# Context rows, first products and the ends of two mixer projections in another order, in a two-layer block

## The reference

```python
silu_c, silu_cc = silu(c), silu(c_ctx)
for i in range(2):                               # layer 0: attention, layer 1: Fourier mixing
    sh1, sc1, g1, sh2, sc2, g2 = split(silu_c @ ada_w[i] + ada_b[i], 6)       # six vectors of 2048
    h = modulate(rms_norm(x, norm_mix_g[i]), sh1, sc1)                        # x: 256 x 2048
    if i == 0:
        h_ctx = modulate(rms_norm(ctx, norm_mix_g[0]), csh1, csc1)            # context: 256 x 2048
        q, k, v = project_qkv(h, attn_w_qkv);  k_c, v_c = project_kv(h_ctx, attn_w_qkv[:, 2048:])
        o = latent_attention(rope(q), rope(k), v, k_c, v_c) @ attn_w_o        # 16 heads, 4 for k and v
    else:
        o = fourier_mix(h) @ fourier_w_o                                      # 8 groups of 256 channels
    x = x + g1 * o
    x = x + g2 * square(relu(modulate(rms_norm(x, norm_mlp_g[i]), sh2, sc2) @ mlp_w1[i])) @ mlp_w2[i]
return rms_norm(x, final_norm_g)
```

## Time and profile before

| | us |
|---|---|
| median of 3 runs (lowest, highest) | 2068.01 (2066.21, 2069.05) |
| the profiled execution | 2064.34 |
| its span, first to last instruction | 2062.5 |
| TensorE busy (matmuls) | 1995.7 |
| VectorE busy | 1364.1 |
| ScalarE busy | 971.5 |

### The profile page before, as it was taken

How to read it: one execution, slowest core, us unless ns; L and a number is a source line. 1 busy time by engine, 2 the same in 40 slices (tenths; PEclk the granted TensorE clock), 3 DMA queues, 4 the chain that set the end, 5 groups by cost and what they waited for, 6 DMA issues and landing times.

```text
span 2062.5 us, 25228 instructions
## 1 busy us (share of the span) xinstructions
PE 1995.7 (97%) x10356; PEld 1630.1 (79%) x10356; DVE 1364.1 (66%) x1373; ACT 971.5 (47%) x1268; POOL 110.6 (5%) x196
## 2 busy tenths in 40 slices
PE   4999989998999999999999999899999999999998
PEld 2677756687888888888888787788888888888886
DVE  1456888758868788677568778766656555455546
ACT  4433555445455445544444443445445554444444
POOL 1111001100000000000000001000000000000000
PEclk8999999999999999999999999999999999999999
DMA  9799758966989899688678739767776565555553
GB/s 369 275 333 353 272 215 300 342 208 224 342 309 337 329 347 377 224 327 322 213 275 352 265 105 344 265 226 248 253 250 230 186 204 189 199 187 201 207 202 122
DMA packets 153797, 542.81 MB, mean 263 GB/s; under 512 B 9393, under 2 KB 10577, under 8 KB 116177
## 3 DMA queue, kind: packets, MB, share of 16 engines
q1 hardware_dynamic: 120848, 335.77, 46.4%
q0 software_dynamic: 31744, 201.34, 26.4%
q10 hardware_dynamic: 1090, 4.09, 0.5%
HBM read 535.91 MB, written 2.10 MB: 261 GB/s over the span
## 4 chain that ended last, share of the span: by engine, by line
PE 88%; DMA 6%; DVE 4%; ACT 1%; issue 1%; POOL 0%; ACTq 0%; SPq 0%; DVEq 0%; POOLq 0%
PE ps L1797 23%; PE ps L1799 12%; PE ps L1741 11%; PE ps L1744 11%; PE ps L1745 11%; PE ps L1577 4%; PE ps L1578 4%; PE ps L1579 4%; DMA ada_raw<-in_ada_w 3%; DMA raw<-in_fourier_w_o 1%; PE ps L1931 1%; PE ps L1879 1%; PE ps L1618 1%; DVE g_row L1053 1%; DMA c_rows<-in_ctx 1%
## 5 line engine op out<-in xcount | busy, mean ns | idle before, releaser
L1025 DVE TENSOR_TENSOR w_lo<-raw,w_hi 128x1024 fp32r<-128x1024 f32 x616 | 748.5, 1222 | 530.6 <-ACT w_hi L624 530.4
L624 ACT ACTIVATE w_hi<-raw 128x1024 fp32r<-128x1024 f32 x616 | 648.7, 1059 | 867.7 <-PE ps L1745 345.4
L1797 PE MATMUL ps<-hh,w_hi 128*128 128x512 f32 x2048 | 723.8, 399 | 3.1 <-DVE hh L1390 3.1
L1799 PE MATMUL ps<-hh,w_lo 128*128 128x256 f32 x2048 | 573.6, 280 | 0.0
L1797 PEld LDWEIGHTS ps<-hh,w_hi 128*128 128x128 f32 x2048 | 386.4, 189 | 100.0 <-issue 7.0
L1799 PEld LDWEIGHTS ps<-hh,w_lo 128*128 128x128 f32 x2048 | 387.8, 189 | 0.0
L1741 PE MATMUL ps<-w_hi,hh 128*128 128x512 f32 x992 | 386.2, 389 | 0.4 <-DVE w_lo L1025 0.4
L1745 PE MATMUL ps<-w_hi,hh 128*128 128x512 f32 x992 | 385.9, 389 | 0.0
L1744 PE MATMUL ps<-w_lo,hh 128*128 128x512 f32 x992 | 385.9, 389 | 0.0
L1741 PEld LDWEIGHTS ps<-w_hi,hh 128*128 128x128 f32 x992 | 186.2, 188 | 39.9 <-DVE w_lo L1025 1.3
L1745 PEld LDWEIGHTS ps<-w_hi,hh 128*128 128x128 f32 x992 | 186.2, 188 | 38.9
(11 more groups left out here) (216 smaller groups left out, 1422.2 us busy)
## 6 DMA issues: line engine op xcount, KB each, us to landing
raw<-in_mlp_w SPq DMA_DIRECT2D x256, 1024.0 KB, 5.3
ada_raw<-in_ada_w POOLq DMA_DIRECT2D x151, 1024.0 KB, 6.0
spare<-in_ada_w POOLq DMA_DIRECT2D x30, 1024.0 KB, 7.1
raw<-in_attn_w_qkv SPq DMA_DIRECT2D x24, 1024.0 KB, 10.6
raw<-in_attn_w_o SPq DMA_DIRECT2D x16, 1024.0 KB, 6.4
raw<-in_fourier_w_o SPq DMA_DIRECT2D x16, 1024.0 KB, 8.5
g_row<-in_ada_w POOLq DMA_DIRECT2D x11, 1024.0 KB, 9.4
g_row<-gate_rows SPq DMA_DIRECT2D x48, 64.0 KB, 5.0
```

The costliest lines, as they stand in the source:

```text
L624: act.activation(w_slot(s)[0], raw[:, piece % RAW, s % 2, :], ACT.Copy).then_inc(hi_ready, 1)
L1025: nc.vector.tensor_tensor(lo, raw[:, s // 2 % RAW, s % 2, :], hi.bitcast(F32), ALU.subtract).then_inc(lo_ready, 1)
L1797: mm(ps[:, bank, :].rearrange("p (a t) -> p a t", a=2), w_hi[:, s % SPLIT, w], hh[:, k, :, :], start=(k == 0), stop=False, skip_group_chec ...
L1799: ins = mm(ps[:, bank, 0:T], w_lo[:, s % SPLIT, w], h_hi[:, k, :], start=False, stop=(k == KT - 1), skip_group_check=True)
```

## The change

It changes the order of work at the start and at two ends, and loads a table earlier.

First stage: the context rows are loaded after weight piece 1 instead of piece 0, and GpSimd waits for them before ada_w piece 8. The ada_w pieces stand after other products for the first quarter, their banks are 6, 6, 7, 6, and the context is turned after product 4 in banks 5 and 7. ScalarE makes split 0 first, then shapes x in two halves, then split 1, and TensorE's products can start on the first half. The context's squares, roots and norms move to p = 1, around splits 4 and 5, and the copies of the turned context on VectorE go behind low parts 6 and 7.

Table: a square root of one column, not used, ahead of split 59.

Ends of the two mixer projections: laying out and picking the vector go behind the last product, on either side of tile 0's turns; VectorE takes it up between the last total and its reciprocal; one low part instead of two stands ahead of the last gate, the other behind the first `h_split`.

```diff
@@ -60,7 +60,8 @@
-ADA_AFTER = (1, 2, 4, 5, 7, 8, 10, 11)
+ADA_AFTER = ((2, 3, 4, 6, 7, 9, 10, 11), (1, 2, 4, 5, 7, 8, 10, 11), (1, 2, 4, 5, 7, 8, 10, 11))
+ADA_BANK = (6, 6, 7, 6)
@@ -331,6 +332,8 @@
     gate_in = sem("gate_in")
+    hhi_first = sem("hhi_first")
+    h_first = sem("h_first")
     pick_ready = sem("pick_ready")
@@ -490,7 +493,7 @@
             load_columns(p, wqkv_v[p // 6, column_block(p)])
-            if p == 0:
+            if p == 1:
                 sp.dma_start(c_rows[:, :, :], ctx_in[0].rearrange("(a p) d -> p a d", p=P)).then_inc(ctx_rows_in, 16)
@@ -545,6 +548,8 @@
                 pool.wait_ge(ada_mm, n - 6)
+            if n == 8:
+                pool.wait_ge(ctx_rows_in, 16)
             dst = ring(start_slot(n)).rearrange("p (k c) -> p k c", k=4)
@@ -669,7 +674,18 @@
                 act.wait_ge(col_mm, g)
-            act.activation(ada_rows[:, :], ps[:, 6 + g % 2, :], ACT.Copy).then_inc(rows_copied, 1)
+            act.activation(ada_rows[:, :], ps[:, ADA_BANK[g], :], ACT.Copy).then_inc(rows_copied, 1)
+
+        def shape_first():
+
+            act.wait_ge(a_ready, 1)
+            for half in range(2):
+                kts = slice(2 * half, 2 * half + 2)
+                for kt in range(2 * half, 2 * half + 2):
+                    act.activation(xT[:, kt, :], xT[:, kt, :], ACT.Identity, bias=mod_col[:, kt:kt + 1],
+                                   scale=a_col[:, 0, kt:kt + 1]).then_inc(mod_done, 1)
+                act.wait_ge(mod_done, 2 * half + 2)
+                act.activation(h_hi[:, kts, :], xT[:, kts, :], ACT.Copy).then_inc((hhi_first, hhi_ready)[half], 1)
@@ -727,19 +743,22 @@
         rows_out(0)
-        shape(0, 0)
         split_hi(0)
+        shape_first()
         split_hi(1)
-        for st in range(2, 4):
-            square_in(st)
-            root_in(st)
         split_hi(2)
...
             g, i = p // 6, p % 6
+            if p == 1:
+                square_in(2)
+                root_in(2)
             if p:
...
                 split_hi(2 * p + 3)
+            if p == 1:
+                square_in(3)
+                root_in(3)
             if g < 3 and i == 5:
@@ -826,6 +845,7 @@
                 q_roots(2, 2)
+        act.activation(rst_in[:, 0, 0:1], eps_col[:, 1:2], ACT.Sqrt)
         split_hi(59)
@@ -882,14 +902,16 @@
             else:
-                if q == 2:
-                    act.wait_ge(rows_T, LAID[8] - 5)
-                    act.activation(ada_rows[:, :], ps[:, 2, :], ACT.Copy).then_inc(rows_copied, 1)
                 square_banks(q, 6, 1)
...
                 split_hi(next_first + 1)
+            if q == 0:
+                rows_early(2)
+            if q == 2:
+                act.wait_ge(rows_T, LAID[8] - 5)
+                act.activation(ada_rows[:, :], ps[:, 2, :], ACT.Copy).then_inc(rows_copied, 1)
             square_banks(q, 7, 1)
@@ -925,8 +947,6 @@
                         square_banks(0, i // 8 * 2 + i % 2, 1)
-                    if i == 9:
-                        rows_early(2)
             else:
@@ -1135,7 +1155,7 @@
                 dve.wait_ge(vec_ready, 3)
-            cols = ps[:, 6 + g % 2, 0:16].rearrange("p (m f h v) -> p v m h f", f=2, m=2, h=2, v=2)
+            cols = ps[:, ADA_BANK[g], 0:16].rearrange("p (m f h v) -> p v m h f", f=2, m=2, h=2, v=2)
             for v, dst in enumerate((mod_col, modc_col)):
@@ -1145,6 +1165,13 @@
                                                misc[:, V_MIX + 4 * g:V_MIX + 4 * g + 4], ALU.add, ALU.mult).then_inc(a_ready, 1)
+
+        def lower_first(half):
+
+            kts = slice(2 * half, 2 * half + 2)
+            dve.wait_ge((hhi_first, hhi_ready)[half], 1)
+            nc.vector.tensor_tensor(h_lo[:, kts, :], xT[:, kts, :], h_hi[:, kts, :].bitcast(F32),
+                                    ALU.subtract).then_inc((h_first, h_ready)[half], 1)
@@ -1224,26 +1251,29 @@
         split_lo(0)
+        lower_first(0)
+        lower_first(1)
         split_lo(1)
-        lower(0, 0)
-        total_in(2)
-        normed_in(2)
-        total_in(3)
-        normed_in(3)
         split_lo(2)
...
             g, i = p // 6, p % 6
+            if p == 1:
+                total_in(2)
+                normed_in(2)
+            if p and p != 20:
+                split_lo(2 * p + 2)
+                split_lo(2 * p + 3)
+            if p == 1:
+                total_in(3)
+                normed_in(3)
             if p == 2:
...
                     nc.vector.tensor_copy(ctxT[:, 2 * k:2 * k + 2, :],
-                                          ps[:, 4 + k % 2, :].rearrange("p (a t) -> p a t", a=2)).then_inc(ctx_T_out, 1)
-            if p and p != 20:
-                split_lo(2 * p + 2)
-                split_lo(2 * p + 3)
+                                          ps[:, 5 + 2 * (k % 2), :].rearrange("p (a t) -> p a t", a=2)).then_inc(ctx_T_out, 1)
             if p == 3:
@@ -1398,12 +1428,10 @@
                     normed(q, 0, b)
-                if middle:
-                    middle()
                 split_lo(next_first)
-                split_lo(next_first + 1)
                 gate_banks(q, 7, 1)
                 total(q, 1)
+                middle()
                 invert(q, 1)
@@ -1483,9 +1511,6 @@
                         gate_banks(0, i // 8 * 2 + (i - 1) % 2, 1)
-                    if i == 12:
-                        take_early(2)
-                        gain_tm(0, V_MLP, 64, 2)
             else:
@@ -1498,17 +1523,22 @@
             def scales():
-                take_col(v, 2)
-                gain_tm(2, V_MLP + KT, 160, 8)
-
-            stage_end(q, 2 * P_UP[l], scales if l else None)
+                if l == 0:
+                    take_early(2)
+                    gain_tm(0, V_MLP, 64, 2)
+                else:
+                    take_col(v, 2)
+                    gain_tm(2, V_MLP + KT, 160, 8)
+
+            stage_end(q, 2 * P_UP[l], scales)
...
             h_split(q, 0)
+            split_lo(first + 1)
+            h_split(q, 1)
             split_lo(first + 2)
-            h_split(q, 1)
+            h_split(q, 2)
             split_lo(first + 3)
-            h_split(q, 2)
@@ -1587,18 +1617,23 @@
                 pe.wait_ge(x_T_out, 8)
-            elif r < 6:
-                pe.wait_ge(ctx_T_out, 3 + r)
+            elif r == 5:
+                pe.wait_ge(ctx_T_out, 7)
             elif 6 <= r < 22:
...
             hi, lo = (h_hi, h_lo) if tt < 2 else (hc_hi, hc_lo)
-            pe.wait_ge(h_ready, 2 * g + 1 + tt // 2)
+            if r < 10:
+                pe.wait_ge(h_first, 1)
+            else:
+                pe.wait_ge(h_ready, 2 * g + 1 + tt // 2)
             tok = slice((tt % 2) * P, (tt % 2 + 1) * P)
...
                 pe.wait_ge(lo_ready, sl + 1)
+                if r == 0 and k == 2:
+                    pe.wait_ge(h_ready, 1)
                 ins = three(ps[:, product_bank(r), :], hi[:, kt, tok], lo[:, kt, tok], w_hi[:, sl % SPLIT, w], w_lo[:, sl % SPLIT, w],
@@ -1608,14 +1643,14 @@
             pe.wait_ge(ada_in[slot], 16 * start_count(n))
-            if g >= 2 and q == 0:
-                pe.wait_ge(start_mods, 4 * (g - 2) + 4)
+            if g and q == 0:
+                pe.wait_ge(start_mods, 4 * g if g == 1 else 4 * g - 4)
             w = ring(slot).rearrange("p (k h c) -> p k h c", k=4, h=2)
...
                     j = 32 * (2 * (k % 2) + h)
-                    ins = mm(ps[j:j + 32, 6 + g % 2, m * T:(m + 1) * T], silu[:, 4 * q + k, :], w[:, k, h, :],
+                    ins = mm(ps[j:j + 32, ADA_BANK[g], m * T:(m + 1) * T], silu[:, 4 * q + k, :], w[:, k, h, :],
                              start=(q == 0 and k < 2), stop=(q == 3 and k >= 2), skip_group_check=True)
@@ -1623,7 +1658,7 @@
             for f in range(4):
-                ins = mm(ps[:, 6 + g % 2, 4 * f:4 * f + 4], ada_rows[:, f * P:(f + 1) * P], pick[:, :], start=True, stop=True)
+                ins = mm(ps[:, ADA_BANK[g], 4 * f:4 * f + 4], ada_rows[:, f * P:(f + 1) * P], pick[:, :], start=True, stop=True)
             ins.then_inc(col_mm, 1)
@@ -1689,10 +1724,6 @@
                     block_unit(q, 6 + tt, k)
-                    if q == 2 and tt == 0 and k == KT - 1:
-                        lay_rows(8, 2)
-                    if q == 2 and tt == 1 and k == 11:
-                        pick_cols(8, 2)
@@ -1826,26 +1857,26 @@
             pe.wait_ge(xn_made, 7 + i // 4)
+            if i == 1:
+                pe.wait_ge(vec_ready, 3)
             if i >= 2:
...
                     f = 2 * i + k
-                    ins = nc.tensor.transpose(ps[:, 4 + i % 2, k * T + tt * P:k * T + (tt + 1) * P], c_rows[:, tt, f * P:(f + 1) * P],
+                    ins = nc.tensor.transpose(ps[:, 5 + 2 * (i % 2), k * T + tt * P:k * T + (tt + 1) * P], c_rows[:, tt, f * P:(f + 1) * P],
                                               ident[:, :])
...
             product(r)
-            if r == 3:
+            if r == 4:
                 for i in range(8):
...
```

(25 more changed lines are left out.)

## The result

The changed kernel takes 2053.2 us (median, 2051.7 to 2055.05) against 2067.48 (2066.21 to 2069.05) for the kernel before, a ratio of 0.9941 with a 95% interval of 0.9923 to 0.9959. By that ratio it is 12.2 us faster, from 8.5 to 15.9; the two medians lie 14.3 us apart. The profiled execution took 2051.7 us, with a span of 2049.9.

The account below looks back on a forecast made before the run. Only shortening TensorE's idle time or taking work out of its full stretches was to move the end. First stage 6.7, attention end 3.8 and Fourier end 1.1 sum to 11.6 us: 2068.0 - 11.6 = 2056.4, range 2049.5 to 2063.

Parts of the forecast that it names:

- (d): First stage: context squares, roots, norms between splits 3 and 6; TensorE loses 1.9 us waiting on context copies; gain 6.7 us.
- (a): First stage's start: context rows behind weight piece 1, GpSimd's ada_w piece 8 waiting for them; split 0 starts at 36.
- (b): Start: split 0 first, x shaped in halves; product 0 starts at about 39.4 instead of 47.23, second half at 42.7.
- (c): First stage: splits 2 and 3 no longer behind the context; product 2 at 47.8 instead of 57.51, 8.6 us ahead.
- rival B: First stage: weight piece 3 lands late beside ada_w pieces, TensorE waits; stage gain 1 to 3, time 2061.5; chance 0.13.
- Rival D: Slower kernel through weight piece 3 landing late; first stage's gain gone at 64.2, whole sum at 69.1; chance 0.04.
- (f) to (i): Attention projection end: fold and pick moved, 1.8 us; earlier table load and one low part fewer, less new waits, 2.0.
- (g): Attention end: square root's table loaded ahead of split 59, just hidden; the root comes 1.06 us earlier.
- (i): Attention end: two small VectorE operations wait for the pick; second normalising still 1.8 earlier; gain 2.0, bounds 0 and 2.5.
- (j) to (l): Fourier projection end: 1.8 us taken out of a full stretch, 0.7 lost behind the last product; gain 1.1 us.
- Rival A: TensorE's clock stays up at one end, or the wait on context copies is small: 4 us more, 2052; chance 0.15.
- Rival C: Whole change: earlier start given back by transfers, ends gain 4.9 less 1.5 of clock: 2064.5; chance 0.08.

## Why the prediction was right

The time, 2053.2, lies 3.2 us under the forecast of 2056.4 and well inside the range; the gain of 12.2 (13.8 the second time) stands beside the forecast's 11.6. By the yardsticks it is 6.0 + 4.1 + 1.4 = 11.5. That this meets the forecast so closely is in part luck: the first stage brought 0.7 less than its term and the two ends 0.3 more each, and inside the first stage two larger errors all but cancelled (see (d)). The forecast leaned on the median shown and not on the profiled execution, and that was needed: the pace of one up stage alone moves one execution by over 4 us.

- **(a), (b), the start: right.** Weight piece 0 landed 0.85 us earlier than taken, product 0 began at 38.78 (39.4), its second half at 41.86 (42.7). The wait on GpSimd does what step (a) says: without it piece 0 took 13.2 us instead of 6.2.
- **(c), product 2: right.** No idle time behind product 1, product 2 at 46.4 (47.8). With the old order it waited until 52.2. It was 11.1 us earlier, 10.1 less the ada_w piece, where 8.6 were forecast.
- **(d), the new wait: its loss put too small, and in the wrong place.** This is the step that failed. It foresaw 1.9 us lost on the context's copies, and said that ada_w piece 8 would be there when product 2 ends. Product 2 ended at 49.2, and the piece landed at 52.13, 8.7 us after its issue beside two others of its queue and three weight pieces (2 to 4). No term of the sum priced that transfer, though a row at hand gave a price (20.0 us for such a piece among others). TensorE lost 2.94 us there and some 1.7 at the low clock (0.4 in the ada_w piece, 1.3 in product 3), and then found the copies almost ready. The two losses are alternatives, not a sum: where the piece came in time, the copies' wait appeared, at 1.96 and 2.79 us in two kernels (and at 4.32 in a third, where weight piece 3 was late too). So the chain that step (d) described was there, behind a wait that it had left out. In numbers: the changed kernel was 10.1 us ahead at product 2 and 6.0 at low part 24, so 4.1 us were lost between them where the sum had 1.9. Step (c) had been 1.5 too low (8.6 against 10.1) and (d) 2.2 too low in its loss, and the first stage came out at 6.0 for 6.7.
- **Weight piece 3 and rival B: right to be hidden.** It took 6.5 us and not 13. Step (d) gave it the row of a weight piece beside three ada_w pieces; in fact it ran ahead of them, as piece 8 was issued 1.5 us later and moved its first packets another 3 us after that, and the 13.0 us of that row held a start of 3.7 us in which its queue moved nothing (next point). Rival B happened in the kernel that let ada_w go earlier, with 17.7 us and a gain of 3.4 in the first stage, a little above its 1 to 3. Rival D was never near: in the changed kernel the piece landed at 48.3, and even with 17.7 us, in that other kernel, at 59.65, before the 64.2 at which the stage's gain would be gone.
- **The queue's share: a third and not a quarter, and its reading wrong.** The prediction took a quarter for the weight queue from the whole 13.0 us of weight piece 0 and wrote that the trace does not agree with the Trainium skill, DMA: Bandwidth & Descriptors, section Queues, rings and completion order, by which each DMA engine takes a packet from each queue row in turn. But for the first 3.7 of these 13.0 us (29.5 to 33.2) the weight queue moved nothing at all. In stretches in which weights (q1) and ada_w (q0) both move, the traces agree with the Trainium skill. These are the DMA queues (packets, MB, share of 16 engines) of the kernel before in 33.5 to 37, of the kernel that waits for weight piece 0 in 44.5 to 52, and of the changed kernel in 48.5 to 52:

```profile
q0 software_dynamic: 222, 0.91, 67.7%
q1 hardware_dynamic: 221, 0.45, 35.9%
```

```profile
q0 software_dynamic: 494, 1.89, 66.1%
q1 hardware_dynamic: 494, 0.98, 36.1%
```

```profile
q0 software_dynamic: 232, 0.88, 65.7%
q1 hardware_dynamic: 233, 0.48, 37.0%
```

  222 of what the profile counts as packets stand against 221, 494 against 494, and 232 against 233; but a packet of the ada_w queue carries 3.8 to 4.1 KB and one of the weights 2.0 (1.89 and 0.98 MB by 494). So the weights get a third of the bytes, as their packets are half as large. It turns round where they are larger: in the kernel before, in 40 to 44, the context rows' packets were 7.8 KB, and with 140 packets against ada_w's 136 that queue moved 1.09 MB against 0.56. Halves of the bytes, as the prediction worked them out from the rule, were its own error.
- **(f) to (i), the attention end: right.** The stretch fell by 2.3 us (forecast 2.0), with the 1.8 of the moved fold and pick 4.1 against 3.8. The table is worth 1.06, the very number of step (g). The two small operations waited 0.24 us for the pick and put the reciprocal 0.50 us after the start of the root, against 0.33 in the kernel without the early table: 0.2 us, nearly hidden, as (i) had it.
- **(j) to (l), the Fourier end: right, a little small.** The loss was 0.37 instead of 0.7, the gain 1.4 instead of 1.1. The chain behind the last product is now the attention end's, to the hundredth of a us.
- **The clock at the ends: right, at nothing.** It fell at both as before (0.72 in 468 to 474, 0.65 in 1332 to 1338). At the attention end it was 0.50 from 469.2 to 472.6, half as long as before (473.7 to 480.5), but there the second turns had stood in it too, and in the repetition of the changed kernel it was 0.51 from 465.4 to 472.3. From the start of its first matmul to that of its hundred and first the up stage took 20.9 and 21.7 us in the trace before, 22.1 and 21.1 in its repetition, and 20.8, 21.8, 22.2 and 20.9 in the two of the changed kernel: a spread of 1.4 us and no shift. From the attention end's last product to the up stage's hundredth matmul, the three traces with the old end took 30.3 to 31.5 us and the eleven with the new one 27.9 to 29.3: some 2.4 us less on average, as the yardstick's 2.3. Rival A's four microseconds are not there.
- **Rival C fell** in the two kernels with half of the change: the parts add up to the whole.

What stays open: whether the ends bring more than their 5.5 us (the timing of the ends alone says 5.6 to 12.2; the stretches above show no place for it), and what sets the pace of the up stage.

## What to carry to other kernels

Holding back a queue that isn't yet needed can halve the landing time of the transfer that everything waits for, but the queue held back becomes the next wait: price its first transfer beside all that is then in flight, as it was done here for the weights and not for ada_w. When one wait is removed, look for the chain that runs beside it; here two waits of 2 to 3 us covered each other, and only removing both moved the stage. For parts of a few us, measure a stretch that comes out the same in every trace, since one span moved by 5 us without any change in the program.
